# Ring slots in halves, row turning on VectorE, an earlier gather index, and a scatter without unused slots in a mixture-of-experts loop

## The reference

```python
def moe_ffn(h, w_router, b_router, w_gu, b_gu, w_down, b_down):
    logits = (x @ w_router) + b_router
    top_v, top_e = lax.top_k(logits, TOP_EXPERTS)          # 4 of 32
    gates = jax.nn.softmax(top_v, axis=-1)
    ...
    def expert_block(args):
        xe, e = args
        gu = xe @ w_gu[e] + b_gu[e]                        # 1024 -> 2048
        gate = jnp.minimum(gu[:, :D_EXPERT], SWIGLU_LIMIT)
        up = jnp.clip(gu[:, D_EXPERT:], -SWIGLU_LIMIT, SWIGLU_LIMIT)
        act = (up + 1.0) * gate * jax.nn.sigmoid(SWIGLU_ALPHA * gate)
        return act @ w_down[e] + b_down[e]                 # 1024 -> 1024
    ...
    y = jnp.zeros((N + 1, D_MODEL)).at[slot_tok].add(yb * slot_gate[:, None])[:N]
```

## Time and profile before

| | us |
|---|---|
| median of three runs | 1653.48 |
| the profiled execution: its own time | 1653.29 |
| its span, first to last instruction | 1651.8 |
| TensorE busy (its share of the span) | 1615.7 (98%) |
| VectorE busy | 609.4 (37%) |
| ScalarE busy | 302.4 (18%) |
| GpSimd busy | 204.7 (12%) |

### The profile page before, as it was taken

The page is one execution under the profiler, slowest core; times in us unless marked ns, Lnnn a source line. Parts: engine busy times, 40 slices in busy tenths (PEclk is TensorE's granted clock), DMA queues, the critical chain, the costliest instruction groups (busy, mean ns, idle before and its releaser), DMA issues. The chain is left out here.

```text
span 1651.8 us, 33511 instructions
## 1 busy us (share of the span) xinstructions
PE 1615.7 (98%) x13818; PEld 763.7 (46%) x13818; DVE 609.4 (37%) x1186; ACT 302.4 (18%) x618; POOL 204.7 (12%) x267
## 2 busy tenths in 40 slices
PE   9999999999998999999999999999999999999996
PEld 7677587786745333333333333333333333333332
DVE  4359549403315333323233233323333233323333
ACT  1310120017112111112111211121111211111112
POOL 3624300015000010000000000000000000000000
PEclk9999999999998899999999999999999999999996
DMA  7456646621454699999999999999999999999963
GB/s 239 145 171 215 230 150 217 214 76 74 172 205 158 229 397 395 392 401 398 393 395 390 402 389 400 386 399 395 392 390 396 399 392 403 386 398 395 398 261 114
DMA packets 70505, 510.01 MB, mean 309 GB/s; under 512 B 11310, under 2 KB 11758, under 8 KB 45230
## 3 DMA queue, kind: packets, MB, share of 16 engines
q1 hardware_dynamic: 60070, 485.28, 74.0%
q0 software_dynamic: 10384, 24.06, 6.2%
HBM read 491.61 MB, written 22.37 MB: 311 GB/s over the span
## 5 line engine op out<-in xcount | busy, mean ns | idle before, releaser
L1209 PE MATMUL PS<-weight_ring,region_experts 128*32 128x512 f32 x6144 | 680.2, 594 | 2.6 <-issue 1.7
L1209 PEld LDWEIGHTS PS<-weight_ring,region_experts 128*32 128x32 f32 x6144 | 200.5, 110 | 413.3 <-issue 410.4
L1216 PE MATMUL PS<-weight_ring,act_turned 128*32 128x512 f32 x2048 | 232.2, 594 | 0.0
L834 PE MATMUL PS<-region_x,region_w 128*128 128x260 f32 (+1 forms) x928 | 209.4, 385 | 0.9 <-DVE region_x L1415 0.9
L834 PEld LDWEIGHTS PS<-region_x,region_w 128*128 128x128 f32 x928 | 175.2, 190 | 31.8 <-issue 3.4
L1536 DVE TENSOR_TENSOR region_experts<-region_experts,region_x 128x640 bf16<-128x640 f32 x33 | 27.2, 825 | 402.0 <-DMA region_experts<-b_gu 402.0
L1216 PEld LDWEIGHTS PS<-weight_ring,act_turned 128*32 128x32 f32 x2048 | 63.3, 110 | 137.7 <-issue 134.0
L616 POOL DMA_INDIRECT y_acc<-region_x,idx_i x32 | 46.9, 1465 | 641.5 <-issue 641.5
L1222 PE MATMUL PS<-weight_ring,act_turned 128*32 128x256 f32 x2048 | 122.2, 379 | 0.0
L1222 PEld LDWEIGHTS PS<-weight_ring,act_turned 128*32 128x32 f32 x2048 | 66.6, 110 | 71.2 <-issue 38.3
L600 POOL DMA_INDIRECT region_x<-h_rows,idx_i x33 | 33.5, 1014 | 431.8 <-DVE idx_i L1551 352.3
(11 more groups left out here) (266 smaller groups left out, 1301.8 us busy)
## 6 DMA issues: line engine op xcount, KB each, us to landing
weight_ring<-w_gu SPq DMA_DIRECT2D x128, 2048.0 KB, 13.8
weight_ring<-w_down SPq DMA_DIRECT2D x64, 2048.0 KB, 16.6
region_w<-w_mt SPq DMA_DIRECT2D x33, 512.0 KB, 4.4
weight_ring<-cache_kT SPq DMA_DIRECT2D x64, 256.0 KB, 4.0
weight_ring<-cache_v SPq DMA_DIRECT2D x64, 256.0 KB, 4.0
weight_ring<-w_out SPq DMA_DIRECT2D x2, 2048.0 KB, 10.7
weight_ring<-bias_strip SPq DMA_DIRECT2D x1, 2560.0 KB, 13.1
region_x<-xT SPq DMA_DIRECT2D x4, 536.0 KB, 7.0
```

The costliest lines, as they stand in the source:

```text
L834: mm = pe.matmul(PB[j % 2][:, a, 0:width], lhs(k), rhs(k)[:, width * a:width * a + width], start=(k == 0), stop=(k == nk - 1))
L1209: mm = pe.matmul(out[GRP * j:GRP * j + GRP], hTe[:, k, GRP * g:GRP * g + GRP], weights(c)[:, k, :], start=(k == 0), stop=(k == KD - 1))
L1216: pe.matmul(bank(3)[GRP * j:GRP * j + GRP], actT[:, k, GRP * g:GRP * g + GRP], w_dn[:, k, 512 * q:512 * q + 512], start=(k == 0), stop=(k ...
```

## The change

- The third round releases slots 1 and 3 in halves: after its first four of eight steps a new semaphore `third_half` counts up, and SP loads the first half (8 KB of each partition) of slot 1 and of slot 3; the second halves follow after the third round. Each half is one transfer of 1 MB, so slots 1 and 3 count 32 in place of 16. The first expert's loads of these slots come in halves too.
- The next expert's rows are turned by VectorE: twelve 32x32 block transposes of 32 partitions x 256 elements, from the gathered rows straight to `hTe`, at the end of VectorE's expert. `hTe` has two buffers. TensorE's eight transposes and ScalarE's copy go; only the first expert is still turned by TensorE.
- The index is copied for the scatter (`keep`, to `idx_y`), so the tile `idx_i` is free earlier, and VectorE waits for the scatter before that copy and no longer before the index.
- The scatter gets the bounds check of the gather.

SP in the loop over the experts, before and after. The first load in each piece is slot 2's; then come slots 1 and 3 (w_gu), the bias rows (b_gu) and slot 4 (w_down). 128x4096 is a whole slot, 128x2048 a half.

The diff, without the declarations of tiles and semaphores, and without the same edits in the passage ahead of the loop:

```diff
+            def half_load(c, z, e):
+                src = w_gu[bass.ds(e, 1), c].rearrange("a p x -> (a p) x")
+                at = RING // 2 * z
+                sp.dma_start(W6[:, slot(c) + at:slot(c) + at + RING // 2], src[:, at:at + RING // 2]).then_inc(r_full[c], 16)
...
                     sp.wait_ge(S["round_done"], (b * NE + e - 1) * ROUNDS + 2)
                     ring_load(2, e)
+                    sp.wait_ge(S["third_half"], b * NE + e)
+                    half_load(1, 0, e)
+                    half_load(3, 0, e)
                     sp.wait_ge(S["round_done"], (b * NE + e - 1) * ROUNDS + 3)
-                    ring_load(1, e)
-                    ring_load(3, e)
+                    half_load(1, 1, e)
+                    half_load(3, 1, e)
...
+                        po.wait_ge(S["idx_kept"], b * SELS + e + 1)
                         po.wait_ge(S["y_ready"], b * NE + e + 2)
                         po.sem_inc(S["pool_may"], 1)
-                        po.indirect_dma_start(y_acc, bass.IndirectOffsetOnAxis(ap=idx_i[u][0:CAP, :], axis=0),
-                                              ysc[u][0:CAP], None, compute_op=ALU.add).then_inc(scat[u], 16)
+                        po.indirect_dma_start(y_acc, bass.IndirectOffsetOnAxis(ap=idx_y[u][0:CAP, :], axis=0),
+                                              ysc[u][0:CAP], None, bounds_check=NQ - 1, oob_is_err=False, compute_op=ALU.add).then_inc(scat[u], 16)
...
                         act.activation(actT[:, 4:8, 0:64], tA[:, :, 0:64], ACT.Copy).then_inc(S["actT_ready"], 1)
-                        hTe_out(b * SELS + e + 2)
...
                         pe.wait_ge(r_full[0], (ne + 1) * 16)
-                        pe.wait_ge(r_full[1], (ne + 1) * 16)
+                        pe.wait_ge(r_full[1], (ne + 1) * 32)
                         pe.wait_ge(S["hTe_ready"], b * SELS + e + 1)
...
-                        gu_round(bank(2), rest, range(6))
+                        gu_round(bank(2), u, rest, range(4)).then_inc(S["third_half"], 1)
+                        gu_round(bank(2), u, rest, range(4, 6))
...
-                        if u == 0:
-                            turn_rows(b * SELS + e + 2, b * (NE // 2) + i + 1, 1)
-                        else:
-                            turn_rows(b * SELS + e + 2, b * (NE // 2 + 1) + i + 2, 0)
                         pe.wait_ge(S["actT_ready"], ne * 2 + 2)
...
+            def keep(u):
+                dve.tensor_copy(idx_y[u][0:CAP, :], idx_i[u][0:CAP, :]).then_inc(S["idx_kept"], 1)
+
+            def turn_rows(u):
+                rows = xg[u].rearrange("p (k x) -> p k x", k=KD)
+                for g in range(CAP // GRP):
+                    for q in range(4):
+                        ins = dve.transpose(hTe[u][32 * q:32 * q + 32, :, GRP * g:GRP * g + GRP],
+                                            rows[GRP * g:GRP * g + GRP, :, 32 * q:32 * q + 32])
+                ins.then_inc(S["hTe_ready"], 1)
...
-                        if u == 0:
-                            dve.wait_ge(scat[1], (b * (NE // 2) + i + 1) * 16)
-                        else:
-                            dve.wait_ge(scat[0], (b * (NE // 2) + i + 2) * 16)
                         index(b * SELS + e + 2, 1 - u)
...
+                        dve.wait_ge(S["idx_ready"], b * SELS + e + 2)
+                        if u == 0:
+                            dve.wait_ge(scat[1], (b * (NE // 2) + i + 1) * 16)
+                        else:
+                            dve.wait_ge(scat[0], (b * (NE // 2) + i + 2) * 16)
+                        keep(1 - u)
+                        if u == 0:
+                            dve.wait_ge(gath[1], (b * (NE // 2) + i + 1) * 16)
+                        else:
+                            dve.wait_ge(gath[0], (b * (NE // 2 + 1) + i + 2) * 16)
+                        dve.sem_inc(S["turn_may"], 1)
+                        turn_rows(1 - u)
```

## The result

The changed kernel takes 1665.8 us (median of 8 runs, 1660.3 to 1668.3), the kernel before 1654.4 in the same series: ratio 1.0063, interval 1.0052 to 1.0074. It is slower by 0.6%. Forecast were 1655.5 and a range from 1643 to 1662; the direction falls into the class that had 0.35, the size lies outside the range. The profiled executions are 1665.85 and 1653.29 us, 12.56 apart.

A forecast was written before the change was run, and what follows sets the result against it. Slot 1's landing, set by the busiest DMA engine, was taken as the bound. Loop start -0.4, split packets +2.7 and turning -0.1 gave +2.2 on 1653.29, so 1655.5 us; range 1643 to 1662.

The forecast's parts named there:

- the class that had 0.35: The outcome "slower", beyond the 0.2% (3.3 us) that can't be told from no change; chance 0.35.
- rival B: Weight loads: halves or alternate reads of two slots cost more than packet sizes say; 0.27 us an expert, 1660.9 us; chance 0.18.
- What bounds the kernel: Expert loop: slot 1's landing on the busiest DMA engine sets 33.66 us an expert; TensorE alone needs 33.38.
- Turning the rows: TensorE's period falls 0.1 us to 33.28, counting once, -0.1 us; VectorE's twelve transposes at 0.4 us each cost 0.
- the watch list: Signs expected in the new trace, among them TensorE waiting about 0.1 us for ScalarE between the down halves.
- The scatter's unused slots: Scatter: 31 packets fewer an expert, but not on the busiest engine; gain 0, bounds 0 and -0.64 us.
- rival A: Scatter: fewer packets relieve the busiest engine, so TensorE sets the pace at 33.28 us an expert; 1644.2 us; chance 0.25.
- Index and gather: Index made 4 to 5 us earlier, gather with it; same bytes elsewhere in the stream, cost 0.
- The halves: Loads of slots 1 and 3: 16 more packets per engine, 0.09 us an expert, +2.7 us; earlier loop start, -0.4 us.
- The halves' second and third point: Slot 1's halves come first and third, 2.45 us later; at the loop start it lands at 573.4, -0.4 us once.
- the quarter of the forecast: Part of the forecast's own spread, 1652 to 1658 us, over the 1656.8 bound; counted 0.12 towards slower.
- C: VectorE's turning comes late and TensorE waits: at 0.68 us a transpose, +10 us, 1664 us; chance 0.05.

The follow-up runs named there:

- skip alone: Kernel before with one edit, the scatter leaves out the unused slots: 1655.6 us, ratio 1.0000.
- the two pairs: Early against late index, whole loads: with VectorE's turning, all rows scattered, 1660.0 against 1654.9 us; with turning and shorter scatter, 1658.4 against 1654.1 us.
- the kernel cut by partitions: Changed kernel with whole loads, but slots 1 and 3 each loaded behind the third round as two 1 MB transfers split by partitions: 2042.2 us, ratio 1.2346.

## Why the prediction was wrong

Two terms of the sum failed: the halves, priced at 0.09 us an expert, cost 0.28, and the parts priced at nothing did not stay at nothing once they were put together. The sign for rival B, 33.9 us an expert and more, came: 34.07.

What bounds the kernel: right, and sharper than I had it. The landing of slot 1 sets the pace, and its bound is one engine. "The busiest engine should be one that has six rows of every gather and one of the bias rows": the bias row was a part that mattered, and I had it as a note beside the gather's rows, whose part no run tested. Its price was in the earlier trace rows as 0.32 us of engine time a row; that it stretches its neighbours isn't visible there, since nothing ran beside it in that window.

Turning the rows: right, on top of the kernel before. 33.26 us against 33.28; VectorE's transposes 0.43 us against 0.4, cost 0 (turning alone, ratio 0.9997). Only the watch list was off: it had the wait for ScalarE at 0.1 us, and the prediction's own times (four transposes done at 939.25, start possible at 939.75) gave 0.5; measured are 0.47. The scatter's unused slots: right, gain 0 (skip alone, 1.0000); rival A fell with it.

**Index and gather: "the bytes are the same, only elsewhere in the stream: 0" failed.** It costs 4 to 5 us in all, 0.09 and 0.24 us an expert in the two pairs, where the loads are whole. I counted bytes, and the place decides: the gather slows the stream for some 6 us, and in its new place the large packets lose 0.16 to 0.34 us more on each engine and expert than in the old. With the halves in, the same edit changed nothing (1.0062 and 1.0063). I had taken a wait that is removed for something that can't hurt.

**The halves: the price of 0.09 us failed by a factor of three.** Halves alone cost 0.28 us an expert and 6.5 us. I had 6 ns for a split packet and 10 at most, from the time of a 2 KB packet in another phase; in the halves' stream a split costs 14 ns in the median, 0.22 us an expert, and behind the third round in plain order 4 ns. So the mixture of packet sizes goes with about 0.14 us an expert and the early release with the rest. This is rival B, whose 0.27 us an expert and 1660.9 us fit the halves alone (1662.0) almost exactly; that factor of three was a guess, and the fit is luck. What it lacked are the 4 us that come on top of the halves, and they stay open: they are there without the early index (1665.2) and without the shorter scatter (1665.4). The changed kernel without VectorE's turning was not run. The rival's premise, "alternate reads of two slots", isn't borne out: with slot 1 first both halves of slot 1 stand before both of slot 3, and the kernel is as slow (1664.7); in that order behind the third round the halves cost half as much.

The halves' second and third point: "three halves after 566.0, at 573.4" failed. With the first expert 1.3 us late the second halves were issued at 567.5, and slot 1's took 8.6 us to land, at 576.12. The first half, into an almost empty queue, had taken 7.1 us itself, so the two early halves gave less of a start than I had counted. The lead at the second expert was 2.6 us instead of 3.9, and at 0.6 us an expert it was gone by the sixth.

Sum: forecast -0.4 + 2.7 - 0.1. In its place stand, in the profiled executions, +2.8 for the lead that ended sooner, +8.2 for twenty experts at 0.41, +1.4 up to the second expert, +0.2 at the end. The range reached to B and stopped there, because each rival was priced as if the other edits were free. The chances didn't add up quite either: the quarter of the forecast, B, C and the rest make 0.37 for slower, not 0.35.

## What to carry to other kernels

Where one DMA engine ends last, find out what it carries that the others don't, and take that away before touching the large loads; leaving the suspected small transfer out, in one run, tells its whole price. An edit that only moves a transfer can have a price where the stream is full: look at what it is moved beside. Parts that cost nothing alone can cost something together, so price the combination too. A price for a smaller packet that comes from another phase doesn't bound what it costs in a stream that mixes sizes and orders.

## What the runs showed of the hardware

A transfer of 24 KB to four partitions cost a full stream of 2 MB loads at least 0.37 us an expert (33.63 to 33.26). TensorE sets the pace without it and may hide a rest, though not much of one: in the last seven experts slot 1 lands only 0.4 to 0.5 us before TensorE starts. Two transfers of 8 KB to 16 partitions cost 0.29.

Loads that write only 64 partitions run at half speed. From 1130 to 1134 us in the kernel cut by partitions:

```profile
DMA packets 71, 0.90 MB, mean 225 GB/s; under 512 B 16, under 2 KB 16, under 8 KB 16
...
q1 hardware_dynamic: 71, 0.90, 108.0%
```

108.0% x 16 x 4 us over 55 packets of 16 KB are 1257 ns each, against 612 for the same packet in a load of 128 partitions. By the Trainium skill ("SBUF — State Buffer", section "Door 1: The DMA port swizzle") 64 partitions in a row reach 8 of 16 ports, about 218 GB/s. By the Trainium skill ("SBUF — State Buffer", section "Can I just issue two DMAs to hit both halves?") a second transfer to the other half adds only 6%. The 225 GB/s of this window agree with both.

Rows of 4 KB that are gathered slow the whole stream while they run: 262 to 342 GB/s at a busy share near 1, against 416 two microseconds before.
